# Prompt attention's value product: one fp32 matmul in two passes, or three single-pass fp32r matmuls fed by a second exponential and a GpSimd subtraction

## The reference, cut to what matters

```python
def masked_softmax(logits, mask):
    p = jax.nn.softmax(jnp.where(mask, logits.astype(jnp.float32), NEG), axis=-1)
    return p * mask
...
    o_slc = jnp.einsum('bgnts,bgtsd->btgnd', ps, vs)   # selected keys: for this prompt, all earlier keys
...
    pw = masked_softmax(lw, mask_w)                    # window of the last 512 keys
    o_win = jnp.einsum('bgnts,bsgd->btgnd', pw, vw)
```

## Time and profile before

| | us |
|---|---|
| median of 3 runs | 3396.54 (3392.3 to 3404.24) |
| the profiled execution | 3395.37 |
| its span, first to last instruction | 3393.6 |
| PE busy | 2877.3 (85%), PEld 2478.3 |
| DVE busy | 1198.8 (35%) |
| ACT busy | 745.2 (22%) |
| POOL busy | 153.2 (5%) |
| L2497, the value products, 264 passes | 142.3, 623 ns each |
| mean granted TensorE clock | 0.895 |

### The profile page before, as it was taken

One profiled execution on the slowest core, in us unless ns is written; L12 is line 12 of the kernel. 1 busy time (PEld: TensorE's weight loads), 2 busy tenths in 40 slices (PEclk: granted clock), 3 DMA queues, 4 the chain that ended last, 5 costly groups with the idle time before them and its releaser, 6 DMA issues. The chain is left out here.

```text
span 3393.6 us, 49040 instructions
## 1 busy us (share of the span) xinstructions
PE 2877.3 (85%) x21498; PEld 2478.3 (73%) x21498; DVE 1198.8 (35%) x2065; ACT 745.2 (22%) x1125; POOL 153.2 (5%) x212
## 2 busy tenths in 40 slices
PE   5898788865898789957589999898665999999998
PEld 4894588752697455534478888797444999999998
DVE  5434544324332556626311111343224222222222
ACT  3212222100113244422210101221212222212211
POOL 0000222100201000011000000000000000000000
PEclk7996899955899699978799999998787999999999
DMA  4510000013511000035521111310120111111111
GB/s 156 205 41 9 4 3 3 3 15 100 130 44 41 1 1 1 1 140 200 208 63 47 38 47 41 105 31 14 55 70 21 49 49 44 44 50 44 44 50 58
DMA packets 178822, 192.34 MB, mean 57 GB/s; under 512 B 18126, under 2 KB 162754, under 8 KB 173377
## 3 DMA queue, kind: packets, MB, share of 16 engines
q1 hardware_dynamic: 168097, 127.16, 12.5%
q0 software_dynamic: 9888, 61.87, 5.2%
q10 hardware_dynamic: 624, 0.18, 0.0%
HBM read 165.52 MB, written 28.00 MB: 57 GB/s over the span
## 5 line engine op out<-in xcount | busy, mean ns | idle before, releaser
L675 PE MATMUL ps<-xf_h,ff_high 128*128 128x352 f32 x768 | 248.7, 324 | 23.2 <-DVE ff_low L664 23.2
L3538 PE MATMUL ps<-ff_hidden_high,ff_high 128*128 128x352 f32 x768 | 249.2, 325 | 4.8 <-issue 4.8
L3540 PE MATMUL ps<-ff_hidden_high,ff_low 128*128 128x352 f32 x768 | 249.0, 324 | 0.0
L3539 PE MATMUL ps<-ff_hidden_low,ff_high 128*128 128x352 f32 x768 | 249.0, 324 | 0.0
L676 PE MATMUL ps<-xf_l,ff_high 128*128 128x352 f32 x768 | 247.2, 322 | 0.0
L677 PE MATMUL ps<-xf_h,ff_low 128*128 128x352 f32 x768 | 247.2, 322 | 0.0
L675 PE MATMUL ps<-xn_h,me_high 128*128 128x352 f32 x576 | 192.7, 335 | 9.3 <-DVE me_low L664 9.3
L676 PE MATMUL ps<-xn_l,me_high 128*128 128x352 f32 x576 | 185.3, 322 | 0.0
L677 PE MATMUL ps<-xn_h,me_low 128*128 128x352 f32 x576 | 185.1, 321 | 0.0
L3582 DVE TENSOR_TENSOR x<-x,ps 128x1056 f32<-128x1056 f32 x64 | 80.2, 1254 | 236.1 <-PE ps L3540 236.0
L675 PEld LDWEIGHTS ps<-xf_h,ff_high 128*128 128x128 f32 x768 | 144.8, 189 | 23.8 <-DVE ff_low L664 23.8
(11 more groups left out here) (675 smaller groups left out, 6426.1 us busy)
## 6 DMA issues: line engine op xcount, KB each, us to landing
ff_raw<-in_w_ff SPq DMA_DIRECT2D x64, 512.0 KB, 4.0
me_raw<-in_w_in SPq DMA_DIRECT2D x24, 512.0 KB, 4.3
pj_raw<-in_w_in SPq DMA_DIRECT2D x13, 512.0 KB, 5.3
xn_high<-xn_h POOLq DMA_DIRECT2D x1, 4224.0 KB, 12.2
xn_low<-xn_l POOLq DMA_DIRECT2D x1, 4224.0 KB, 23.7
xn_h<-xn_high POOLq DMA_DIRECT2D x1, 4224.0 KB, 13.7
xn_l<-xn_low POOLq DMA_DIRECT2D x1, 4224.0 KB, 23.8
xn_h<-xn_high SPq DMA_DIRECT2D x1, 4224.0 KB, 13.3
```

The lines of the kernel that those rows point to most:

```text
L675: e.matmul(o, W.hi[:, z, k, :], rh[:, k, n], start=k == ks[0], stop=False)
L3538: e.matmul(o, W.hi[:, u % NSPL, 2 * k + z, :], hh[:, r, ns], start=k == 0, stop=False)
L3539: e.matmul(o, W.hi[:, u % NSPL, 2 * k + z, :], hl[:, r, ns], start=False, stop=False)
L3540: mm = e.matmul(o, W.lo[:, u % NSPL, 2 * k + z, :], hh[:, r, ns], start=False, stop=k == GB - 1)
```

## The change

The exponential is taken twice by ACT for each tile: into `PH` rounded to fp32r, then into `PT` in full fp32. POOL computes `PL = PT - PH` in fp32r, in place: `PL` is allocated at the address of `PT`. `va` becomes fp32r (rounded by POOL's copies), and POOL makes its low part `vl` at the stage's start with a small and two large subtractions. The value product becomes three fp32r matmuls into the same bank: `va` x `PH`, `vl` x `PH`, and after a wait for POOL (`s_low`) `va` x `PL`. PE waits once for `vl` ahead of the first unit's scores. To make room in SBUF, `PH` and the small tiles of the stage are laid over memory of `tail` and `utail`; therefore DVE and ACT wait near the stage's start for the stores that read `tail`, for which only SP waited before, at the stage's end. `vc` moves into the stage before. The memset of the ones becomes a copy.

```diff
--- before.py
+++ after.py
@@ -2176,14 +2176,14 @@
             low_block(e, W, 7)
 
 
-def stage_nsa_keys(nc, K, qT, kvt, kcd, vc, kh, kl, ksn, kwn, near, nearT, cb, b31, va, vbd, EP, ES, tail):
+def stage_nsa_keys(nc, K, qT, kvt, kcd, kh, kl, ksn, kwn, near, nearT, cb, b31, va, vbd, EP, ES, tail):
 
 
     scale = 0.125
     ctx = ExitStack()
     with ctx:
         sb = lambda nm, sh: ctx.enter_context(nc.sbuf_tensor("nk_" + nm, sh, F32))
-        kc, sq, rt = sb("kc", [P, 16]), sb("sq", [P, 16]), sb("rt", [P, 16])
+        vc, kc, sq, rt = sb("vc", [16, P]), sb("kc", [P, 16]), sb("sq", [P, 16]), sb("rt", [P, 16])
         qsq, qrt, spread = sb("q_sq", [P, 2, T]), sb("q_root", [32 * NC3, NW]), sb("q_to_channels", [32 * NC3, 4 * P])
         block = ctx.enter_context(nc.Block())
         s_t, s_c, s_new, s_m, s_sq, s_s, s_v, s_r = (K.sem("nk_" + x) for x in (
@@ -2270,7 +2270,8 @@
             for b in range(DB):
                 e.dma_start(K.d["s_state_pool"][0, b, 15 - DT:15, :].rearrange("t (b n) -> t b n", n=P),
                             tail[15 + DT * b:15 + DT * b + DT, B_POOL:B_Q, :]).then_inc(s_prow, 16)
-            e.memset(va[:, :, :, :, 64:65], 1.0)
+            one = K.c("ones")[:, 0:32].rearrange("p (z i g d) -> p z i g d", z=2, i=NTI, d=1)
+            e.tensor_copy(va[:, :, :, :, 64:65], one)
             for z in range(2):
                 e.tensor_copy(va[:, z, :, :, 0:64], kvt[:, 0:NTI, 384 + 256 * z:512 + 256 * z].rearrange("p i (g d) -> p i g d", g=2))
             for g in range(4):
@@ -2355,7 +2356,7 @@
                                        ALU.mult, ALU.mult).then_inc(s_qu, 1)
 
 
-def stage_nsa_prompt(nc, K, qT, kvt, kcd, va, vbd, kh, kl, near, nearT, cb):
+def stage_nsa_prompt(nc, K, qT, kvt, kcd, va, vbd, kh, kl, near, nearT, cb, tail_at):
 
 
     units = [(i, g) for i in range(NTI) for g in range(2)]
@@ -2414,18 +2415,23 @@
         sb = lambda nm, sh, d=F32: ctx.enter_context(nc.sbuf_tensor("np_" + nm, sh, d))
         QA = sb("query_parts", [P, 2, 8, P], F32R)
         QB = sb("query_shift", [P, 2, 512], F32R)
+        PL = nc.alloc_sbuf_tensor_at("np_probs_low", [P, NPT, 512], F32R, offset=nc.sbuf_base)
         PT = sb("probsT", [P, NPT, 512])
+        over = lambda nm, sh, at, d=F32: nc.alloc_sbuf_tensor_at("np_" + nm, sh, d, offset=at)
+        PH = over("probs_high", [P, NPT, 512], tail_at, F32R)
+        vl = sb("values_low", [P, 2, NTI, 2, 65], F32R)
         OT = sb("outT", [65, 2, 512])
-        O = sb("out", [P, 2, 4, 64])
-        mx, nm = sb("maxes", [P, 2, 4, 2, 3]), sb("negmax", [P, 2, 4, 2])
-        co = sb("coef", [P, 2, 4])
-        sc, cT = sb("cmp_scores", [P, 8, 16]), sb("cmpT", [P, 2, P])
-        cm, cs = sb("cmp_max", [P, 8]), sb("cmp_sum", [P, 8])
+        O = over("out", [P, 2, 4, 64], K.utail_at)
+        mx, nm = over("maxes", [P, 2, 4, 2, 3], K.utail_at + 3072), over("negmax", [P, 2, 4, 2], K.utail_at + 3264)
+        co = over("coef", [P, 2, 4], K.utail_at + 3328)
+        sc, cT = over("cmp_scores", [P, 8, 16], tail_at + 8192), over("cmpT", [P, 2, P], K.utail_at + 2048)
+        cm, cs = over("cmp_max", [P, 8], tail_at + 8704), over("cmp_sum", [P, 8], tail_at + 8736)
         block = ctx.enter_context(nc.Block())
         s_qh, s_ql, s_clear, s_qb, s_look, s_seen, s_nm, s_cr = (K.sem("np_" + x) for x in (
             "queries_high", "queries_low", "shift_cleared", "shift_ready", "looked", "seen", "max", "shift_turned"))
         s_sc, s_add, s_exp, s_val, s_evac, s_turn, s_scaled, s_fin, s_fe = (K.sem("np_" + x) for x in (
             "scores", "biased", "exps", "values", "values_out", "turned", "scaled", "final", "final_out"))
+        s_low, s_vl = K.sem("np_probs_low_set"), K.sem("np_values_low_set")
         s_ca, s_ce, s_cp = (K.sem("np_cmp_" + x) for x in ("shifted", "exps", "weighted"))
 
         @block.tensor
@@ -2494,7 +2500,11 @@
                 e.wait_ge(s_exp, G + 1)
                 if first and u >= 1:
                     e.wait_ge(s_evac, 2 * (u - 1) + z + 1)
-                e.matmul(K.ps[0:65, 2 + z, :], va[:, z, j, g, :], PT[:, G % NPT, :], start=first, stop=j == i).then_inc(s_val, 1)
+                o = K.ps[0:65, 2 + z, :]
+                e.matmul(o, va[:, z, j, g, :], PH[:, G % NPT, :], start=first, stop=False)
+                e.matmul(o, vl[:, z, j, g, :], PH[:, G % NPT, :], start=False, stop=False)
+                e.wait_ge(s_low, G + 1)
+                e.matmul(o, va[:, z, j, g, :], PL[:, G % NPT, :], start=False, stop=j == i).then_inc(s_val, 1)
 
             def turn(u):
                 e.wait_ge(s_evac, 2 * u + 2)
@@ -2520,6 +2530,7 @@
             for c in range(len(looks(0))):
                 look(0, c)
             shift(0)
+            e.wait_ge(s_vl, 1)
             for u in range(NU):
                 at, when = plan(u)
                 for k in range(len(when)):
@@ -2632,6 +2643,8 @@
                 e.tensor_tensor(O[:, :, :, :], got[:, :, :, 0:64], co[:, :, :].unsqueeze(3).to_broadcast([P, 2, 4, 64]),
                                 ALU.mult).then_inc(s_scaled, 1)
 
+            e.wait_ge(K.out_sem("tail_stored"), 16 * K.tail_stores)
+            e.wait_ge(K.out_sem("pool_rows_stored"), 16 * (1 + DB))
             e.tensor_scalar(QB[64:128, :, :].rearrange("p b (h n) -> p (b h) n", n=P),
                             K.c("ident")[64:128, :].unsqueeze(1).to_broadcast([64, 8, P]), 0.0, None, ALU.mult).then_inc(s_clear, 1)
             e.memset(mx[:, :, :, :, :], 3 * NEG)
@@ -2687,11 +2700,13 @@
                 kind, j = tiles(i)[k]
                 if shade(i, kind, j):
                     e.wait_ge(s_add, adds[G])
+                    e.activation(PH[:, G % NPT, :], PT[:, G % NPT, :], ACT.Exp)
                     e.activation(PT[:, G % NPT, :], PT[:, G % NPT, :], ACT.Exp).then_inc(s_exp, 1)
                 else:
                     e.wait_ge(s_sc, G + 1)
                     if G >= NPT:
                         e.wait_ge(s_val, G - NPT + 1)
+                    e.activation(PH[:, G % NPT, :], K.ps[:, G % 2, :], ACT.Exp)
                     e.activation(PT[:, G % NPT, :], K.ps[:, G % 2, :], ACT.Exp).then_inc(s_exp, 1)
 
             def evacuate(G):
@@ -2753,6 +2770,18 @@
             e.wait_ge(K.out_sem("tail_stored"), 16 * K.tail_stores)
             e.wait_ge(K.out_sem("kv_rows_stored"), 16 * 2 * DB)
             e.wait_ge(K.out_sem("pool_rows_stored"), 16 * (1 + DB))
+
+        @block.gpsimd
+        def _(e):
+            one = K.c("ones")[:, 0:32].rearrange("p (z i g d) -> p z i g d", z=2, i=NTI, d=1)
+            e.tensor_tensor(vl[:, :, :, :, 64:65], one, one, ALU.subtract)
+            for z in range(2):
+                mm = e.tensor_tensor(vl[:, z, :, :, 0:64], kvt[:, 0:NTI, 384 + 256 * z:512 + 256 * z].rearrange("p i (g d) -> p i g d", g=2),
+                                     va[:, z, :, :, 0:64].bitcast(F32), ALU.subtract)
+            mm.then_inc(s_vl, 1)
+            for G in range(NG):
+                e.wait_ge(s_exp, G + 1)
+                e.tensor_tensor(PL[:, G % NPT, :], PT[:, G % NPT, :], PH[:, G % NPT, :].bitcast(F32), ALU.subtract).then_inc(s_low, 1)
 
 
 SS, SWN, SCM = PAST + DT, 512 + DT, 32
@@ -3864,6 +3893,7 @@
+        K.utail_at = -(-nc.sbuf_base // 32) * 32
@@ -3930,12 +3960,14 @@
                     ahead = raw_slots(nc, K, c3, "pp", KD, 2)
                     stage_kv(nc, K, kvt, xh2, xl2, near, cb, b31, idx, kv_raw, kv_high1, kv_low1, ahead, order)
                     stage_projections(nc, K, qT, EP, ES, kvt, xh2, xl2, ahead)
+                tail_at = -(-nc.sbuf_base // 32) * 32
                 tail = sc("tail_rows", [TAIL, B_Q, P])
-                kcd, vc = sc("kcd", [P, 2, 16]), sc("vc", [16, P])
+                kcd = sc("kcd", [P, 2, 16])
                 kh, kl = (c2.enter_context(nc.sbuf_tensor(n, [P, 2, 2, TP], F32R)) for n in ("keys_high", "keys_low"))
-                nearT, va, vbd = sc("near_turned", [P, 2, 8, P]), sc("values_ones", [P, 2, NTI, 2, 65]), sc("vc_by_head", [P, 512])
-                stage_nsa_keys(nc, K, qT, kvt, kcd, vc, kh, kl, ksn, kwn, near, nearT, cb, b31, va, vbd, EP, ES, tail)
-                stage_nsa_prompt(nc, K, qT, kvt, kcd, va, vbd, kh, kl, near, nearT, cb)
+                va = c2.enter_context(nc.sbuf_tensor("values_ones", [P, 2, NTI, 2, 65], F32R))
+                nearT, vbd = sc("near_turned", [P, 2, 8, P]), sc("vc_by_head", [P, 512])
+                stage_nsa_keys(nc, K, qT, kvt, kcd, kh, kl, ksn, kwn, near, nearT, cb, b31, va, vbd, EP, ES, tail)
+                stage_nsa_prompt(nc, K, qT, kvt, kcd, va, vbd, kh, kl, near, nearT, cb, tail_at)
             reuse_semaphores()
             with ExitStack() as c2:
                 sc = lambda name, shape: c2.enter_context(nc.sbuf_tensor(name, shape, F32))
```

## The result

The changed kernel takes 3414.7 us, the median of 10 runs (3408.8 to 3417.8); the kernel before takes 3399.3 us on the same chips (10 runs, 3391.7 to 3404.2). The ratio is 1.0045, with an interval of 1.0035 to 1.0055: 15.4 us slower. The forecast was 3390 and the range ended at 3404. The profiled execution of after took 3408.8 us, the lowest of its ten, against 3395.4 of before.

A forecast was written before the change was run, and what follows sets the result against it. PE, with its waits for DVE, was taken as the bound. Terms -23.8 + 3 + 2 + 3.7 + 2 + 3.5 + 2.8 = -6.8 us gave some 3388.6 from 3395.4, named as 3390, range 3376 to 3404.

The forecast's parts named there:

- The bound: Prompt attention stage: PE, busy 309 of 354 us, sets its length, with waits for DVE; a gain passes on.
- The passes, -23.8: Value product on PE: three fp32r passes of 0.23 us a tile instead of 0.86 us save 23.8 us.
- The second exponential, +3: ACT: in short units the shift's copy queues behind a tile's exponential and delays the next scores, 3 us (bounds 0 and 10).
- the rival with the clock: PE at its waits: two or three more half-clock spells, +8 on -6.8, about 3398, no change; chance 0.14.
- The subtraction and its lag, +2 and +3.7: POOL's subtraction takes 1.26 us; PE's lag for the low part costs 2 us from 1210 to 1442, 3.7 in the last unit.
- POOL beside DVE, +2, +3.5 and +2.8: SBUF lock between POOL and DVE: 2 us at the start, 3.5 for seven later pairs, 2.8 for seven compressed-branch endings.
- The first rival: POOL and DVE hardly collide on PE's path and the shift is not late: -18 us, 3378; chance 0.28.
- the gain comes through: POOL-DVE collisions (8.3 us) and the late shift (3 us) stay away, leaving -18 us, 3378; chance 0.28.
- The edits costed at nothing: Wait for `vl`, stores of `tail`, rounded values, `vc`, the ones, moved small tiles: claimed to cost no time.
- The low part is late at every step: PE's third value matmul: POOL at 2.3 us instead of 1.26 bounds the long units, +22, 3419; chance 0.10.
- The signs named for a failure: POOL's instruction over 2 us, PE waiting for it in the middle units, or the stage shortening by 15 us or more.
- the two signs for DVE: DVE's L2549 and L2600 were to show means above 0.69 and 0.29 us.

The follow-up runs named there:

- e3: Changed kernel without POOL's subtractions in the loop, third pass reading the rounded probabilities, and only the rounded exponential: 3381.8 us, ratio 0.9956.
- e6: Changed kernel with two small DVE instructions (compressed scores less maximum, coefficients' multiply) fed from PSUM instead of two SBUF inputs: 3398.9 us, ratio 0.9998.
- e10: Kernel before, POOL idle, with only the edit feeding two small DVE instructions from PSUM: 3406.2 us, ratio 1.0017.
- e1: Changed kernel without POOL's 132 subtractions in the loop; third value matmul reads the rounded probabilities, both exponentials stay: 3388.6 us, ratio 0.9970.
- e2: Changed kernel with POOL's subtractions, but the third value matmul reads the rounded probabilities and PE does not wait for POOL: 3408.4 us, ratio 1.0027.
- e9: Kernel before plus an idle 128x512 POOL subtraction of SBUF data behind each of 132 exponentials, result unused: 3420.1 us, ratio 1.0062.
- e5: Changed kernel, PE not waiting for POOL, each POOL subtraction in the loop replaced by two constant writes that read nothing: 3392.2 us, ratio 0.9976.

## Why the prediction was wrong

*The bound.* Right: PE and its waits for DVE set the stage, and time passed on to the end: after's stage is 14.1 us longer, the profiled execution 13.4.

*The passes, -23.8.* Nearly right. The three passes follow each other at 0.23 us (1473.64 and 1473.87 below). e3 gives -16.6 by medians and -17.9 by stage length; without the start's collision of 3.2 us, -20 to -21.

*The second exponential, +3.* Too small: +7 to +9. The mechanism was wrong too. ACT's shift is not later to speak of (2.7 instead of 1.8 us in one wait, 3.0 instead of 2.4 in another); PE's busy time is 8.5 us up, at a lower clock. That is the rival with the clock, which was priced at +8 and held to be the whole story or nothing. It took place in part, beside the other costs. Why later exponentials lower the granted clock was not tried.

*The subtraction and its lag, +2 and +3.7.* Right: 1.30 us where 1.26 stood, 4 to 6 us in all where 5.7 stood. The last unit goes much as it was walked through, at POOL's pace, 1.26 us from one product to the next where PE would need 1.16:

```profile
1472.90 0.45 PE L2507 MATMUL ps<-np_probs_low,values_ones 128*65 128x512 f32 x1 [0.56 <-POOL np_probs_low L2784]
...
1473.64 0.40 PE L2504 MATMUL ps<-np_probs_high,values_ones 128*65 128x512 f32 x1
1473.87 0.40 PE L2505 MATMUL ps<-np_probs_high,np_values_low 128*65 128x512 f32 x1
...
1474.90 0.40 PE L2504 MATMUL ps<-np_probs_high,values_ones 128*65 128x512 f32 x1
```

*POOL beside DVE, +2, +3.5 and +2.8: here it failed.* The mechanism was the right one, read from one stretched row, and the size was wrong, 6.3 us in the loop against 19 to 20 measured, 2 at the start against 3.2. The step that failed is the list of DVE instructions that POOL can hold: it named the pair and three small ones of the compressed ending, 40 in all, and put two lines with both inputs in SBUF, 24 instructions, at nothing. The first rival's "some 60" seems to count them (by the groups there are 64), the sum does not. Item by item, in DVE's held time:

- the query pairs: 18.4 - 11.0 = 7.4 us, 3.2 of it at the start, so 4.2 in the loop where 3.5 stood. Right.
- the compressed endings, L2606, L2609 and L2611: 1.5 + 1.1 + 0 = 2.6 us where 2.8 stood. Right in sum, but not as it was thought: L2611, which was to show it, was never held.
- the subtraction of the compressed maximum, L2578 (L2567 of before): 4.4 us where nothing stood. It is not in the ending but in `see`, where DVE takes the maxima of the looks, so that the maxima stand behind it. Nor does it come at random: six of its eight come 0.40 to 0.49 us behind the start of a subtraction and wait out the rest, 0.93 to 1.05 us instead of 0.29. The line of L2578 in after (ns, min/median/max; first and last start), and one of the six:

```profile
L2578 DVE TENSOR_TENSOR np_cmp_scores<-np_cmp_scores,np_cmp_max x8: 291/1028/1048, 1129.7 to 1411.2; 128x128 f32<-128x128 f32 x8
```

```profile
1183.77 1.27 POOL L2784 TENSOR_TENSOR np_probs_low<-np_probsT,np_probs_high 128x512 fp32r<-128x512 f32 x1 [0.99 <-ACT np_probsT L2704]
...
1184.26 0.93 DVE L2578 TENSOR_TENSOR np_cmp_scores<-np_cmp_scores,np_cmp_max 128x128 f32<-128x128 f32 x1
```

- the coefficients' multiply, L2639 (L2628 of before): 6.6 us where nothing stood. It has both inputs in SBUF, runs in each of the 16 units, and 10 of the 16 were held. The reciprocal and the product on either side of it read PSUM. It is on the path: L2643 and the next unit's looks stand behind it in DVE's queue.

That is 17.8 us in the loop, 11.0 of them in the two lines that stood at nothing. e6 frees just these two, and its stage is 11.3 us shorter and DVE's busy time 11.3 us less, though the edit alone costs 6.2 us of stage (e10). What was held reached the stage whole, and more: from e1 to e2 15.4 us more in the groups of such instructions, 13.5 us more idle time of PE and 5.5 us more of its busy time. DVE's looks feed PE, and PE has no other work there. The rival "the gain comes through" rested on DVE's slack; that slack was not where these instructions are. The edits costed at nothing cost nothing that a row shows.

*The balance.* The forecast was -6.8 us and after's stage is 14.1 longer, 20.9 apart. By stage lengths 12.4 of these are POOL beside DVE in the loop (18.7 against 6.3), 6.3 the second exponential (9.3 against 3), 2.7 the passes (-21.1 against -23.8), 1.2 the start, and -1.7 the low part's lag (4.0 against 5.7).

*The rivals.* "The low part is late at every step" had named a time that came nearest, 3419, and fell all the same: it wanted POOL at 2.2 us or more, POOL took 1.30, and e9 loses 19 us with no one waiting for POOL's result. The time that agrees is no evidence for the mechanism. The signs named for a failure were two of POOL and one of the stage being shorter; none was for DVE's held time, which is where it was. Of the two signs for DVE that the forecast did name, L2549 grew as it said and L2600 (L2611 of after) did not.

The Trainium skill's page "SBUF — State Buffer", section "SBUF: two separate sides", has the lock hold for DVE with two SBUF inputs only against a GpSimd instruction that reads SBUF. The rows of e5 agree, 139 us of POOL's writes and no instruction held in the loop, and so do those of e9, where POOL reads. By that rule the count would have had to run over every such DVE instruction of the stage, 24 more.

## What to carry to other kernels

Before an engine that seems idle gets work, list from the code every instruction of its neighbour that both can block, the smallest too: a held instruction pays what is left of the one that holds it, whatever its own length, and a 0.17 us multiply paid 0.4 us on the mean and 1.0 at most. Then look at what stands behind each in its queue. Inputs left in PSUM, a turn given to the neighbour first and bulk work moved to the stage before bought back some 24 us here together (ratio 1.0045 to 0.9974), while the same work on the busy neighbour cost more than the collisions (1.0076).

## What the runs showed that was not expected

- The two engines alternate: a DVE pair beside POOL instructions that follow without a gap waits once for each of its two instructions (1.39 to 3.35 and 4.63 us), not once in all.
- POOL's writes alone hold nothing: 264 memsets of 0.53 us, and L2639's and L2577's means stayed at 168 and 292 ns.
- The same 1516 matmuls kept PE busy 284.3 us in e3, 292.7 in e1, 298.2 in e2 and 299.0 in after, at granted clocks of 0.91, 0.89, 0.88 and 0.88. Work that adds nothing to PE can change how fast it runs by 5%. Of the 32.0 us between e3's stage and after's, 14.7 are this, and 17.3 are idle time of PE. Of the 14.7, 8.5 came with the second exponential, 5.5 with POOL's subtractions and 0.8 with the wait for the low part; how these lower the clock was not tried.
